# The stationary operand with the two token blocks interleaved: weight loads that step over every other column

## The reference

```python
xn = rmsnorm(x, norm_w)                    # 256 x 2048
proj = xn @ w_in                           # w_in: 2048 x 18432
(rq, rk, rv, rz, dq, dk, dv, dz, g_ret, g_diff) = split(proj)
o_ret  = rmsnorm(retention(rotary(rq), rotary(rk), rv)) * silu(rz)
o_diff = rmsnorm(diff_attention(rotary(dq), rotary(dk), dv, lam), subln_w) * 0.8 * silu(dz)
mixed = sigmoid(g_ret) * (o_ret @ w_ret_up) + sigmoid(g_diff) * (o_diff @ w_diff_up)
out = rmsnorm(x + mixed @ w_out, final_norm_w)
```

## Time and profile before

| | |
|---|---|
| time, median of 3 runs | 1137.43 us (1137.37 to 1137.45) |
| span of the profiled execution, first to last instruction | 1135.8 us |
| TensorE matmul (PE) busy | 1118.0 us, 98% |
| TensorE weight load (PEld) busy | 925.6 us, 81% |
| VectorE / ScalarE / GpSimd busy | 615.7 / 515.1 / 72.2 us |
| mean granted TensorE clock | 0.999 of full speed |
| main memory | 185 GB/s over the span |

### The profile page before, as it was taken

How to read it: one execution, slowest core, us unless ns; L and a number is a source line. 1 busy time by engine, 2 the same in 40 slices (tenths; PEclk the granted TensorE clock), 3 DMA queues, 4 the chain that set the end, 5 groups by cost and what they waited for, 6 DMA issues and landing times.

```text
span 1135.8 us, 14905 instructions
## 1 busy us (share of the span) xinstructions
PE 1118.0 (98%) x5051; PEld 925.6 (81%) x5051; DVE 615.7 (54%) x729; ACT 515.1 (45%) x664; POOL 72.2 (6%) x76
## 2 busy tenths in 40 slices
PE   6999999999999999999999999999999999999997
PEld 5888888788888888888888888888888888888885
DVE  5655445465544455555655655465555564566544
ACT  5444444444444533444544454445544454444443
POOL 7400000000000000000010001000100010000111
PEclk9999999999999999999999999999999999999999
DMA  8766655666665566666566655665656655666863
GB/s 272 229 183 180 187 169 171 189 188 173 185 179 171 167 206 195 191 186 187 167 182 186 180 171 168 186 184 171 179 180 187 170 182 168 189 186 185 281 214 111
DMA packets 108402, 211.18 MB, mean 186 GB/s; under 512 B 6452, under 2 KB 7496, under 8 KB 107848
## 3 DMA queue, kind: packets, MB, share of 16 engines
q1 hardware_dynamic: 105632, 203.46, 60.4%
q10 hardware_dynamic: 2728, 7.15, 1.7%
HBM read 208.48 MB, written 2.10 MB: 185 GB/s over the span
## 4 chain that ended last, share of the span: by engine, by line
PE 96%; DVE 1%; ACTq 1%; issue 1%; ACT 0%; POOLq 0%; POOL 0%; DVEq 0%
PE bank L836 30%; PE bank L838 30%; PE bank L837 30%; PE bank L845 1%; PE bank L855 1%; PE bank L863 1%; PE bank L864 1%; PE bank L958 1%; PE bank L862 1%; DVE w_lo L558 0%; DVE xt_lo L620 0%; ACTq L360 0%; PE bank L962 0%; PE bank L1011 0%; PE bank L903 0%
## 5 line engine op out<-in xcount | busy, mean ns | idle before, releaser
L558 DVE TENSOR_TENSOR w_lo<-raw,w_hi 128x1024 fp32r<-128x1024 f32 x384 | 478.6, 1248 | 479.2 <-ACT w_hi L376 478.6
L376 ACT ACTIVATE w_hi<-raw 128x1024 fp32r<-128x1024 f32 x384 | 406.9, 1061 | 580.7 <-PE bank L838 569.3
L836 PE MATMUL bank<-w_hi,xt_hi 128*128 128x512 f32 x1280 | 508.4, 397 | 2.3 <-DVE w_lo L558 1.6
L838 PE MATMUL bank<-w_hi,xt_lo 128*128 128x512 f32 x1280 | 499.3, 390 | 0.0
L837 PE MATMUL bank<-w_lo,xt_hi 128*128 128x512 f32 x1280 | 498.6, 390 | 0.0
L836 PEld LDWEIGHTS bank<-w_hi,xt_hi 128*128 128x128 f32 x1280 | 240.7, 188 | 51.3 <-DVE w_lo L558 2.4
L838 PEld LDWEIGHTS bank<-w_hi,xt_lo 128*128 128x128 f32 x1280 | 240.3, 188 | 51.2
L837 PEld LDWEIGHTS bank<-w_lo,xt_hi 128*128 128x128 f32 x1280 | 240.8, 188 | 48.2
L836 PE MATMUL bank<-w_hi,ot_hi 128*128 128x512 f32 x256 | 100.0, 391 | 0.0
L838 PE MATMUL bank<-w_hi,ot_lo 128*128 128x512 f32 x256 | 99.7, 389 | 0.0
L837 PE MATMUL bank<-w_lo,ot_hi 128*128 128x512 f32 x256 | 99.6, 389 | 0.0
(11 more groups left out here) (102 smaller groups left out, 409.4 us busy)
## 6 DMA issues: line engine op xcount, KB each, us to landing
raw<-w_in_dram SPq DMA_DIRECT2D x288, 512.0 KB, 3.8
raw<-w_ret_up_dram SPq DMA_DIRECT2D x32, 512.0 KB, 4.8
raw<-w_diff_up_dram SPq DMA_DIRECT2D x32, 512.0 KB, 4.4
raw<-w_out_dram SPq DMA_DIRECT2D x32, 512.0 KB, 4.7
mixed<-x_dram ACTq DMA_DIRECT2D x4, 512.0 KB, 8.4
gate<-x_dram ACTq DMA_DIRECT2D x1, 2048.0 KB, 10.4
out_dram<-mixed SPq DMA_DIRECT2D x8, 256.0 KB, 2.5
decay_sb<-decay_dram ACTq DMA_DIRECT2D x1, 1024.0 KB, 12.8
```

The source lines that it names most:

```text
L376: act.activation(w_hi[:, s, :, :], raw[:, s, :, :], ACT.Copy).then_inc(hi_ready, 1)
L558: dve.tensor_tensor(w_lo[:, s, :, :], raw[:, s, :, :], w_hi[:, s, :, :].bitcast(F32), ALU.subtract) \
L836: pe.matmul(bank[bk][:, :], hi, w_hi[:, s, kk, :], start=k == 0, stop=False)
L838: return pe.matmul(bank[bk][:, :], lo, w_hi[:, s, kk, :], start=False, stop=k == KT - 1)
```

## The change

The two token blocks of `xt_hi` and `xt_lo` are interleaved: token `t` of block `b` lies at column `2 t + b` of its channel group in place of `128 b + t`. The 24 + 24 instructions that fill the two buffers read their PSUM bank as before and write with a step of two columns; those of VectorE also read `xt_hi` with a step of two. The matmuls of the input and the output projection take a stationary operand of 128 columns with a step of two, which is 8 bytes in place of 4. `ot_hi` and `ot_lo`, the moving operands, the number and the order of the instructions, and every semaphore stay as they are.

```diff
+        def by_block(xt, ks):
+            return xt[:, ks, :].rearrange("p k (t b) -> p k b t", b=BLOCKS)
...
                 for k in (2 * j, 2 * j + 1):
-                    last = act.activation(xt_hi[:, k, :], bank[j][:, (k % 2) * TOKENS:(k % 2 + 1) * TOKENS],
-                                          ACT.Copy, scale=norm_col[:, k:k + 1])
+                    src = bank[j][:, (k % 2) * TOKENS:(k % 2 + 1) * TOKENS].rearrange("p (k b t) -> p k b t", k=1, b=BLOCKS)
+                    last = act.activation(by_block(xt_hi, slice(k, k + 1)), src, ACT.Copy, scale=norm_col[:, k:k + 1])
...
-                act.activation(xt_hi[:, k:k + 2, :], bank[4 + half][:, :].rearrange("p (k t) -> p k t", k=2),
-                               ACT.Copy).then_inc(mt_hi_ready, 1)
+                act.activation(by_block(xt_hi, slice(k, k + 2)),
+                               bank[4 + half][:, :].rearrange("p (k b t) -> p k b t", k=2, b=BLOCKS), ACT.Copy).then_inc(mt_hi_ready, 1)
...
                     last = dve.scalar_tensor_tensor(
-                        out=xt_lo[:, k, :], in0=bank[j][:, (k % 2) * TOKENS:(k % 2 + 1) * TOKENS],
-                        scalar=norm_col[:, k:k + 1], in1=xt_hi[:, k, :].bitcast(F32),
-                        op0=ALU.mult, op1=ALU.subtract)
+                        out=by_block(xt_lo, slice(k, k + 1)), in0=src, scalar=norm_col[:, k:k + 1],
+                        in1=by_block(xt_hi, slice(k, k + 1)).bitcast(F32), op0=ALU.mult, op1=ALU.subtract)
...
-                dve.tensor_tensor(xt_lo[:, k:k + 2, :], bank[4 + half][:, :].rearrange("p (k t) -> p k t", k=2),
-                                  xt_hi[:, k:k + 2, :].bitcast(F32), ALU.subtract).then_inc(drained[4 + half], 1)
+                dve.tensor_tensor(by_block(xt_lo, slice(k, k + 2)),
+                                  bank[4 + half][:, :].rearrange("p (k b t) -> p k b t", k=2, b=BLOCKS),
+                                  by_block(xt_hi, slice(k, k + 2)).bitcast(F32), ALU.subtract).then_inc(drained[4 + half], 1)
...
-                hi, lo = left_hi[:, k, b * P:(b + 1) * P], left_lo[:, k, b * P:(b + 1) * P]
+                if left_hi is ot_hi:
+                    hi, lo = left_hi[:, k, b * P:(b + 1) * P], left_lo[:, k, b * P:(b + 1) * P]
+                else:
+                    hi, lo = (by_block(xt, slice(k, k + 1))[:, 0, b, :] for xt in (left_hi, left_lo))
```

## The result

The changed kernel takes 1159.9 us (median of 4 runs, 1159.62 to 1160.19) against 1137.44 us for the kernel before beside it (1137.37 to 1138.1). The ratio is 1.0196 with a 95% interval of 1.0184 to 1.0208: slower by 22.5 us. The whole interval lies above 1. The forecast was no change, so it was wrong; the time lies inside the range, between "no change" and the rival of a shared read path. The mean granted clock, 0.999 before and 0.998 after, is too nearly the same to explain 2%.

What follows compares the result with a forecast made beforehand. The prediction took the distance between TensorE's matmuls as the bound. It summed 1135.8 us of span, zero for loads, shared path and drains, and 1.6 us from span to median: 1137.4 us, range 1136 to 1189 us.

Steps and rivals of the forecast that it cites:

- no change: Whole kernel: the likeliest case, nothing added, 1137.4 us with its own range of 1136.5 to 1139 us; chance 0.56.
- the rival of a shared read path: Every matmul on `xt`: stepped loads hold up the moving stream, 42 to 50 us more, 1179 to 1188 us; chance 0.27.
- What bounds the kernel: TensorE's chain: the distance between matmuls bounds the time; one nanosecond more on each of 3,840 is 3.8 us, or 0.34%.
- The loads, 3,840 of them: Stationary loads from `xt`: even at half rate, 0.22 us fits into the 0.226 us distance; taken as zero, upper end 111 us.
- A shared read path: Matmuls on `xt`: whether stepped loads enlarge the 0.013 us excess over 0.2133 us; 42 to 50 us possible, taken as zero.
- the load's reads hold up the stream's: Full-rate matmuls on `xt`: a load with columns twice as far apart may hold the stream up twice as much, 42 to 50 us.
- the excess belongs to the full-rate stream alone: Full-rate matmuls on `xt`: the excess stays as it is under the step, adding zero.
- My argument from evenness: Two projection stretches, GpSimd idle or busy: excess equal within a nanosecond or two, which was taken to speak against competing reads.
- The drains: 24 on each of VectorE and ScalarE, writing with a step of two: taken as zero, upper end 3.9 us at the start.
- The load as the bound: Loads on `xt`: the step stretches their pitch from 0.11 us beyond 0.226 us; up to 111 us, up to 1248 us; chance 0.08.
- slow drains: Start of the kernel: strided drains slow, loads not; 2.4 to 3.9 us more, 1140 to 1141 us; chance 0.05.
- a gain: Matmuls on `xt`: the step makes load and stream collide less; at most 42 us less, 1095 us; chance 0.04.

Runs made afterwards that it cites:

- the kernel of 256 columns: Each 512-column projection matmul on `xt` of the changed kernel split into two of 256, each with its own step-two load; 1197.33 us, against 1196.6 us with step one.

## Why the prediction was wrong

**What bounds the kernel: right.** The whole change is in the distance between matmuls on `xt`, and one nanosecond of it is 3.8 us. The 0.226 us that I read from counts and rounded starts is 226.7 to 227.6 ns by the whole nanoseconds. Nothing else moved the time.

**The loads, 3,840 of them: right, with a correction.** I had 0.116 us of cover between loads 0.11 us apart and a distance of 0.226 us. In the changed kernel two such loads behind a short product stand 0.12 us apart (554.97 and 555.09), in the timeline that answers to the earlier trace rows:

```profile
554.97 0.20 PEld L844 LDWEIGHTS bank<-w_hi,xt_hi 128*128 128x128 f32 x1
555.00 0.49 PE L844 MATMUL bank<-w_hi,xt_hi 128*128 128x512 f32 x1
555.06 1.23 DVE L562 TENSOR_TENSOR w_lo<-raw,w_hi 128x1024 fp32r<-128x1024 f32 x1 [1.57 <-ACT w_hi L380]
555.09 0.20 PEld L845 LDWEIGHTS bank<-w_lo,xt_hi 128*128 128x128 f32 x1
```

Step two makes the load's record 7 ns longer, not twice as long, and its closest spacing goes from 110 to 118 ns. Beside a full-rate stream the kernel of 256 columns repeats it every 120 ns, which answers my own doubt, that I had inferred the cover from half-rate streams. So the load did not become the bound. With a step of four it does at 384 columns; at 512 that is open.

**A shared read path: this step failed.** I saw that 0.013 us of each distance were something else, offered two readings, "the load's reads hold up the stream's" and "the excess belongs to the full-rate stream alone", and took the second at zero. The term measured 6.0 ns a matmul, 23 us. Both readings are wrong as I put them. The first was right that the load touches the stream's pace, but it would make the price grow with how much is read and how far apart it lies: a step of three or four adds only 1.1 and 1.8 ns to that of two, and one stationary column costs 230.0 ns. The second would leave the distance alone whatever the load does. The sentence of the Trainium skill, "TensorE: Matmul & The Clock Gate", Part 2, that the next weights take no read bandwidth from the running matmul, is not borne out as a promise that load and stream do not touch: at 512 moving columns the distance changes with the load's place and shape. At 384 columns the means with a step of one and two are 175.3 and 176.5 ns, in different stages, and at 256 columns 121.2 and 121.4, so there the sentence nearly holds. My argument from evenness, that two readers which compete would not give such an equal excess, was the error. The two stretches that I compared differ in what GpSimd does, but both had the same kind of load in the same kind of place, so their evenness could say nothing about load and stream. It was that of a pattern which a change of the load breaks, and the sum took it for a constant of the machine.

**The drains: right.** VectorE's cost nothing. ScalarE's grew by 23 and 37 ns, and the kernel with the strided drains alone is at 1.0002 (0.9992 to 1.0011).

**The rivals.** The shared read path named the place rightly, every matmul on `xt`; its threshold of 0.6 ns was passed tenfold, and its price of 42 to 50 us is twice the measured one. The load as the bound did not occur, nor did slow drains or a gain. That the time lies inside the range is due to this rival's share of it and not to the sum. Two of the prediction's numbers are loose, without effect on the outcome: 1137.4 + 50 is 1187.4 and not 1188 us, and the 2.4 us at the lower end of slow drains is not worked out anywhere.

**What stays open.** Shown is that the stepped loads alone cost the 2%, that the even pattern of 226.7 ns occurred only with the full load of 128 neighbouring columns and both operands at suitable places, that moves by 256 bytes kept it in the two cases tried, and that every other stepped, shortened or moved operand tried at 512 columns gives a mean of 229.9 to 236.6 ns (the last with a step of four in the output projection), apart from one move by 16 bytes. Not shown is the mechanism. That reads of the two operands meet in parts of the memory which repeat every 256 bytes is only argued, and it leaves unexplained why one stationary column with its start in place is also off the pattern.

## What to carry to other kernels

A load of the stationary operand with a step of two float32 is nearly free in its own time, and still the kernel lost 2%, because the distance between full-rate `fp32r` matmuls of 512 columns depends on the place and the shape of both operands. Where a kernel is bound by such matmuls back to back, keep stationary pieces packed, and keep the starts of both operands on a grid of 256 bytes: moves by that much kept the pattern here both times that they were tried. The step cost next to nothing at 256 moving columns, so measure at the length in use. Look at the distances between starts, where an even row of equal numbers is a state that can be lost, and not at the busy share. Bound such a change by the spread of distances that the trace already shows after its breaks (224 to 236 ns here): (236 - 227) x 3840 = 35 us, an estimate that would have covered every mean measured here but the 236.6 ns. No run tests it as a rule, but the kernel before held its own warning.

## What was not expected of the hardware

Loading less can be slower: 64 stationary columns in place of 128 took the distance from 227.4 to 230.1 ns, and one column, over and over, to 231.1. An offset of 4 bytes in a packed operand costs 6 ns a matmul (233.3 against 227.4), with a load's record that is not a nanosecond longer. And the patterns seem to be counted in steps of 6.67 ns, which is 16 cycles at 2.4 GHz: the even ones lie at 120.0, 173.3, 226.7 and 233.3 ns (18, 26, 34 and 35 steps), and 229 + 238 = 467 is 70. No run tells why.
